# One more wait ahead of every second indirect transfer, and four clears behind a norm's powers, in a hybrid encoder on one core

## The chip, the cores and the metric

The kernel runs on one core of one Trainium2 chip. The core has five engines that work beside each other: TensorE (PE, the matmuls), VectorE (DVE), ScalarE (ACT), GpSimd (POOL) and SyncE (SP, which here only issues transfers), and 16 DMA engines that move data between HBM and the on-chip memory. The metric is the device time of one execution in microseconds (us); lower is better. Engines wait for one another through semaphores: counters that an instruction or a transfer raises when it is done.

## The reference, cut to what matters

The program is a two-layer encoder on 256 tokens of width 1024. Each layer has a token mixer (layer 0: windowed attention; layer 1: chunked gMLP) and then a PEER block, a mixture over 16384 experts of which each token uses 16 in each of 8 heads:

```python
def peer(h, w_query, sub_keys, expert_down, expert_up):
    ...
    q = (x @ w_query).reshape(T, PEER_HEADS, 2, D_HALF)
    s = jnp.einsum('thcd,hckd->thck', q, sub_keys).astype(jnp.float32)
    s1, i1 = lax.top_k(s[:, :, 0], PEER_TOPK)
    s2, i2 = lax.top_k(s[:, :, 1], PEER_TOPK)
    cand = (s1[..., :, None] + s2[..., None, :]).reshape(T, PEER_HEADS, PEER_TOPK * PEER_TOPK)
    ...
    top_s, pos = lax.top_k(cand, PEER_TOPK)
    idx = jnp.take_along_axis(cidx, pos, axis=-1)
    gate = jax.nn.softmax(top_s, axis=-1).astype(h.dtype)
    ...
        a = jax.nn.gelu(jnp.einsum('cd,chkd->chk', xc, expert_down[ic]))
        return jnp.einsum('chk,chkd->cd', a * gc, expert_up[ic])
```

## The kernel before, in words

The kernel does not gather experts. It computes the down products of all 16384 experts for all tokens, multiplies them with a matrix of gates that is zero wherever an expert was not chosen, and runs the up product over all experts. The gates lie in HBM, one tensor per layer (`gates`, 128 x 128 x 256 floats, 16.8 MB). It is first cleared by 32 plain transfers of 512 KB that POOL issues (`clear`), and then POOL writes the chosen gates into it by indirect transfers (`scatter`, `indirect_dma_start`). An item is one head of one half of the tokens, so there are 16 items a layer; each item takes 16 indirect transfers, each of one float for each of 128 tokens. That makes 256 indirect transfers a layer and 512 in all.

All weights arrive in **units** of 128 x 1024 floats (512 KB). SP loads a unit into one of four `raw` buffers; ACT makes its high half (`split_hi`, L465), DVE the low half (`split_lo`, L719), PE multiplies with both (three matmuls per product) and raises the semaphore `used` by one when it is through with the unit. Units are counted through the whole program: layer 0 has 20 units for the mixer, 16 for the query, 128 for down and 128 for up; layer 1 has 72, 16, 128 and 128. A query or down unit is 24 matmuls of 256 columns. ACT evicts the product of each query unit (L630) and of each down unit (L646).

While PE works on the query and the down units, DVE finds the 16 best experts of one item after the other (the search, 7 down units an item, until down unit 100), between its `split_lo`s. An item's indirect transfers wait for its gates (`gate_done`) and its addresses (`named`, made by ACT), and for the landing of the item before of the same tokens (`added`). At the end of the down stage SP waits for `added` before it loads the first gates for the up stage.

Ahead of each projection stands an RMS norm. DVE and ACT make the mean square, POOL raises it to the power -1/2 (`root`, L373, one small instruction for each half of the tokens), DVE scales, and PE turns the tiles. POOL is one queue in program order: in layer 0 the two powers of the second norm stand behind all 32 clears, and behind the powers stand the store of `h` to HBM (`h_kept`, L426) and the scatter. DVE's copy of the first key scores (L1085, first of the query stage) waits until that store has landed. Then come the loads for layer 1, which wait for units of the up stage.

What sets the order is thus the program order on each engine and these waits; there is no planner. The functions that the change touches are these.

Of the kernel before, what the change touches and what calls it, by code (L numbers as in the profile page):

```python
# [28 lines left out]
PH, TOPK, NK = 8, 16, 128  # L29
# [8 lines left out]
ZERO_UNITS = 4  # L38
TURN_ORDER = (0, 2, 1, 3, 4, 6, 5, 7)
FILL = 16  # L40
G_TILES = 4
RMS_EPS, LN_EPS = 1e-6, 1e-5
MASKED = -1.0e30
# [8 lines left out]
ATTN_UNITS, SG_V_UNITS, SG_UNITS, QUERY_UNITS = 20, 24, 72, 16  # L52
# [34 lines left out]
def build(nc, x, attn_units, sg_units, query_units, down_units, up_units, sub_keys, rel_table, bucket_map, sink,  # L87
# [5 lines left out]
    with ExitStack() as ctx:  # L93
# [3 lines left out]
        def sem(name):  # L97
            return ctx.enter_context(nc.semaphore(name))
# [16 lines left out]
        sums = sb("sums", [P, 2])  # L115
        g_t = [sb(f"g_t{s}", [P, T]) for s in range(G_TILES)]
        gains = sb("gains", [P, 2 * DEPTH, KD])
# [90 lines left out]
        used = sem("used")  # L208
# [51 lines left out]
        added = [[sem(f"added{n}_{t}") for t in range(TT)] for n in range(DEPTH)]  # L260
        g_landed = [sem(f"g_landed{s}") for s in range(G_TILES)]
        gated_up = sem("gated_up")
# [8 lines left out]
        unit0, p10 = [], []  # L271
# [18 lines left out]
        def _(sp):  # L290
# [24 lines left out]
            for layer in range(DEPTH):  # L315
# [8 lines left out]
                def up_gates(c, i):  # L324
                    sp.wait_ge(gated_up, i * GROUP + (layer * NK + c - G_TILES + 1))
                    sp.dma_start(g_t[c][:, :], gates[layer][bass.ds(i * GROUP + c, 1), :, :].rearrange("o p t -> (o p) t")
# [21 lines left out]
        @block.gpsimd  # L348
        def _(pool):
            pool.memset(ident[:, :], 0.0).then_inc(made, 1)  # L350
            pool.wait_ge(made, 1)
            pool.memset(neg_half[:, :], -0.5).then_inc(made, 1)
            pool.wait_ge(made, 2)
            pool.memset(table[BUCKETS:BUCKETS + 1, :], 1.0).then_inc(made, 1)
            pool.wait_ge(made, 3)
            pool.affine_select(out=ident[:, :], in_=ident[:, :], compare_op=ALU.not_equal, fill=1.0,
                               base=0, pattern=[[-1, P]], channel_multiplier=1).then_inc(made, 1)
            pool.memset(zeros[:, :], 0.0).then_inc(made, 1)
            pool.iota(token[:, :], [[1, 1]], base=0, channel_multiplier=1,
                      allow_small_or_imprecise_dtypes=True).then_inc(made, 1)  # L360
            pool.iota(place[:, :], [[1, TOPK]], base=0, channel_multiplier=0,
                      allow_small_or_imprecise_dtypes=True).then_inc(made, 1)
            pool.dma_start(gains[:, :, :], mix_g).then_inc(const_landed, 16)
            pool.dma_start(sink_in, sink.partition_broadcast(P)).then_inc(const_landed, 16)
            n = [0]

            def root(t):

                n[0] += 1
                if n[0] > 1:  # L370
                    pool.wait_ge(rstd_done, n[0] - 1)
                pool.wait_ge(ms_done, n[0])
                pool.tensor_tensor(stat[:, 1, t], stat[:, 0, t], neg_half[:, t], ALU.pow).then_inc(rstd_done, 1)  # L373

            def roots():
                for t in range(TT):
                    root(slice(t, t + 1))

            def load_keys(layer):
                pool.dma_start(keys_t.rearrange("p n k -> p (n k)"), sub_keys[layer]).then_inc(keys_landed, 16)  # L380

            def clear(layer, chunks, at):

                for q in chunks:
                    pool.wait_ge(used, at(q))
                    pool.dma_start(gates[layer][ZERO_UNITS * q:ZERO_UNITS * q + ZERO_UNITS].rearrange("i p t -> p i t"),  # L386
                                   zeros[:, :].rearrange("p (o t) -> p o t", o=1).broadcast_to([P, ZERO_UNITS, T])
                                   ).then_inc(zeroed, 16)

            def scatter(layer):  # L390

                pool.wait_ge(zeroed, 16 * (layer + 1) * (NK // ZERO_UNITS))
                flat = bass.AP(gates[layer].tensor, 0, [[1, NK * P * T], [1, 1]])
                for m in range(ITEMS):
                    t, head = m % TT, m // TT
                    pool.wait_ge(gate_done, ITEMS * layer + m + 1)
                    pool.wait_ge(named, ITEMS * layer + m + 1)
                    if head:
                        pool.wait_ge(added[layer][t], 16 * TOPK * head)
                    for k in range(TOPK):  # L400
                        pool.indirect_dma_start(flat, bass.IndirectOffsetOnAxis(address[:, TOPK * m + k:TOPK * m + k + 1], 0),  # L401
                                                whole[:, t, head, k:k + 1], None, element_offset=P * t
                                                ).then_inc(added[layer][t], 16)

            roots()

            pool.wait_ge(bias_row_done, 1)
            pool.dma_start(bias_rows, bias_row_sb[0:HEADS, :]).then_inc(bias_stored, 16)
            pool.wait_ge(bias_stored, 16)
            pool.dma_start(bias, bass.AP(bias_rows.tensor, 0, [[1, P], [4 * P, HEADS], [1, KEYS]])  # L410
                           ).then_inc(bias_landed, 16)
            pool.wait_ge(used, 8)
            load_keys(0)
            pool.wait_ge(made, 7)
            for layer in range(DEPTH):
                if layer == 0:
                    clear(0, range(NK // ZERO_UNITS), lambda q: 7 + 13 * q // 32)
                else:
                    roots()
                    at = unit0[1]["mix"]  # L420
                    clear(1, range(8), lambda q: at + 2 + 2 * q)
                    root(slice(0, TT))
                    clear(1, range(8, 32), lambda q: at + SG_V_UNITS + 4 + q)
                roots()
                pool.wait_ge(h_done, 4 * (2 * layer + 1))
                pool.dma_start(h_kept, h.rearrange("p t d -> p (t d)")).then_inc(h_stored, 16)  # L426
                scatter(layer)

                up = unit0[layer]["up"]
                if layer == 0:  # L430
                    at = up + HALF
                    for q in range(4):
                        c = slice(q * FF // 4, (q + 1) * FF // 4)
                        for where, what in ((g_bc[:, c], ln_g[c].partition_broadcast(P)),
                                            (b_bc[:, c], ln_b[c].partition_broadcast(P)),
                                            (wsp.rearrange("p j q -> p (j q)")[:, c],
                                             w_spatial.rearrange("p j q -> p (j q)")[:, c])):
                            pool.wait_ge(used, at)
                            pool.dma_start(where, what).then_inc(sg_landed, 16)  # L439
                            at += 3  # L440
                    for q in range(4):
                        c = slice(q * FF // 4, (q + 1) * FF // 4)
                        pool.wait_ge(used, at)
                        pool.dma_start(bsp.rearrange("p j q -> p (j q)")[:, c], b_spatial[c].partition_broadcast(P)
                                       ).then_inc(sg_landed, 16)
                        at += 3
                    pool.wait_ge(used, up + KEYS_COLUMN + 16 * NK // T)
                    load_keys(1)
                for t in range(TT):
                    pool.wait_ge(used, up + H_COLUMN + (t + 1) * (D // T))  # L450
                    pool.dma_start(h[:, t, :], h_kept[:, t * D:(t + 1) * D]).then_inc(h_landed, 16)  # L451
                if layer:
                    pool.dma_start(gain_row, final_g.partition_broadcast(P)).then_inc(gain_landed, 16)
            roots()
# [253 lines left out]
        def _(dve):  # L708
# [72 lines left out]
            for layer in range(DEPTH):  # L781
# [416 lines left out]
                def gate(n, i=0):  # L1198

                    dve.wait_ge(g_landed[n % G_TILES], i * 16 + 16 * (layer * NK // G_TILES + n // G_TILES + 1))  # L1200
                    a = acts[:, bass.ds(i * GROUP + n, 1), :]
                    dve.tensor_tensor(a, a, g_t[n % G_TILES][:, :].rearrange("p (o t) -> p o t", o=1), ALU.mult  # L1202
                                      ).then_inc(gated_up, 1)
# [84 lines left out]
        def _(pe):  # L1288
# [39 lines left out]
            def fill(bank):  # L1328

                for k in range(FILL):  # L1330
                    pe.transpose(psum[:, bank, P * (k % 4):P * (k % 4) + P], x_lo[:, k % KD, P:T].bitcast(F32), ident[:, :])
# [283 lines left out]
```

## Time and profile before

| | |
|---|---|
| median of 3 runs | 2186.74 us (2177.4 to 2198.01) |
| the profiled execution's own time | 2200.02 us |
| its span | 2198.2 us |
| PE busy | 1969.8 us, 90% |
| DVE busy | 1381.5 us, 63% |
| ACT busy | 1005.4 us, 46% |
| POOL busy | 664.3 us, 30% |
| mean granted TensorE clock | 0.934 of full |

Busy time of PE is modelled and overlaps itself; at a busy PE of 90% there may still be time in which few matmuls start. The page's slices split the span in 40 parts of 55 us. "Issue" as a releaser is time in which the engine waited for nothing that the profile shows, and "another core or an unknown queue" is a releaser that the profile can't name. On one core the latter is some queue or sequencer of the same core.

### The profile page before, as it was taken

The numbers are of one execution on the slowest core, as the hardware profiler recorded it, in microseconds if no ns is written. First come the engines' busy times: TensorE is split into PE (matmuls) and PEld (weight loads), VectorE is DVE, ScalarE is ACT, GpSimd is POOL, SyncE is SP. The second block draws the span as 40 slices with busy tenths as digits, with TensorE's granted clock in tenths as the row PEclk, the third lists the DMA queues.
The fourth block names the chain that finished last, engine by engine and source line by source line (L and its number), as shares of the span: only waits on it lengthen the run. The fifth ranks groups of instructions, "written<-read, shape, count | busy, mean of one in ns | idle before, by whom it ended". The sixth has DMA issues, their size and how long they took to land.

```text
span 2198.2 us, 38688 instructions
## 1 busy us (share of the span) xinstructions
PE 1969.8 (90%) x12114; PEld 1769.0 (80%) x12114; DVE 1381.5 (63%) x2970; ACT 1005.4 (46%) x1638; POOL 664.3 (30%) x627
## 2 busy tenths in 40 slices
PE   7978788777979999999999988789688799999998
PEld 6777688777979888888889988689588798888887
DVE  6856466456635766676567766467466535667776
ACT  5633354334535455444434444445254344554454
POOL 2324656656720000000102024666745620000000
PEclk9988898788989999999999998799798999999999
DMA  6943344333536877888749743344243356777775
GB/s 223 384 151 119 121 144 137 113 118 122 172 124 203 253 243 245 290 287 267 247 158 318 258 145 121 110 150 150 93 144 124 122 165 221 243 241 240 242 242 195
DMA packets 159588, 419.97 MB, mean 191 GB/s; under 512 B 32428, under 2 KB 66252, under 8 KB 159021
## 3 DMA queue, kind: packets, MB, share of 16 engines
q1 hardware_dynamic: 130556, 369.23, 52.1%
q0 software_dynamic: 28976, 50.17, 6.7%
q8 instruction: 16, 0.26, 0.1%
q14 instruction: 40, 0.32, 0.0%
HBM read 382.30 MB, written 37.00 MB: 191 GB/s over the span
## 4 chain that ended last, share of the span: by engine, by line
PE 77%; issue 7%; another core or an unknown queue 6%; ACT 5%; DVE 3%; DMA 2%; POOL 0%; SPq 0%; DVEq 0%; POOLq 0%; ACTq 0%
PE psum L1291 25%; PE psum L1293 25%; PE psum L1292 24%; ACT w_hi L465 2%; DVE w_lo L719 1%; ACT L614 1%; DMA big<-bias_rows 1%; PE psum L1490 1%; ACT L656 1%; PE psum L1461 1%; PE psum L1390 0%; PE psum L1379 0%; PE psum L1416 0%; DMA raw<-in_attn_units 0%
## 5 line engine op out<-in xcount | busy, mean ns | idle before, releaser
L719 DVE TENSOR_TENSOR w_lo<-raw,w_hi 128x1024 fp32r<-128x1024 f32 x636 | 772.5, 1219 | 452.4 <-ACT w_hi L465 341.2
L1291 PE MATMUL psum<-x_hi,w_hi 128*128 128x256 f32 x2576 | 767.0, 298 | 116.1 <-issue 68.5
L465 ACT CAST w_hi<-raw 128x1024 fp32r<-128x1024 f32 x636 | 662.5, 1047 | 345.1 <-PE psum L1293 328.1
L1292 PE MATMUL psum<-x_lo,w_hi 128*128 128x256 f32 x2576 | 753.7, 293 | 36.9 <-issue 36.4
L1293 PE MATMUL psum<-x_hi,w_lo 128*128 128x256 f32 x2576 | 754.1, 293 | 30.3 <-issue 29.7
L401 POOL DMA_INDIRECT gates<-whole,address x512 | 590.5, 1153 | 418.3 <-DVE whole L1073 167.3
L1291 PEld LDWEIGHTS psum<-x_hi,w_hi 128*128 128x128 f32 x2576 | 517.6, 201 | 142.5 <-issue 97.3
L1292 PEld LDWEIGHTS psum<-x_lo,w_hi 128*128 128x128 f32 x2576 | 518.8, 201 | 41.5 <-issue 40.4
L1293 PEld LDWEIGHTS psum<-x_hi,w_lo 128*128 128x128 f32 x2576 | 517.9, 201 | 39.5 <-issue 39.5
L1291 PE MATMUL psum<-w_hi,l_hi 128*128 128x512 f32 x1152 | 452.6, 393 | 3.4 <-DVE l_lo L1218 2.2
L1293 PE MATMUL psum<-w_hi,l_lo 128*128 128x512 f32 x1152 | 449.2, 390 | 0.0
L1292 PE MATMUL psum<-w_lo,l_hi 128*128 128x512 f32 x1152 | 449.0, 390 | 0.0
L646 ACT ACTIVATE big<-psum 128x256 f32<-128x256 f32 x256 | 98.1, 383 | 556.0 <-PE psum L1293 279.4
L1291 PEld LDWEIGHTS psum<-w_hi,l_hi 128*128 128x128 f32 x1152 | 216.9, 188 | 49.2 <-issue 4.4
L1293 PEld LDWEIGHTS psum<-w_hi,l_lo 128*128 128x128 f32 x1152 | 216.7, 188 | 45.8
L1292 PEld LDWEIGHTS psum<-w_lo,l_hi 128*128 128x128 f32 x1152 | 216.9, 188 | 43.8
L1207 DVE TENSOR_TENSOR l_lo<-big,l_hi 128x256 fp32r<-128x256 f32 x248 | 105.5, 426 | 190.7 <-ACT l_hi L664 190.7
L451 POOL DMA_DIRECT2D big<-h_kept x4 | 2.2, 551 | 418.8 <-PE psum L1293 418.8
L1202 DVE TENSOR_TENSOR big<-big,g_t 128x256 f32 (+1 forms) x248 | 104.0, 419 | 8.1 <-DMA g_t<-gates 8.1
L386 POOL DMA_DIRECT2D gates<-zeros x64 | 48.1, 755 | 183.3 <-PE psum L1293 160.4
L664 ACT CAST l_hi<-big 128x256 fp32r (+1 forms) x248 | 98.0, 396 | 0.0
L439 POOL DMA_DIRECT2D big<-in_ln_g x4 | 2.2, 548 | 270.1 <-PE psum L1293 270.1
(143 smaller groups left out, 1133.0 us busy)
## 6 DMA issues: line engine op xcount, KB each, us to landing
raw<-in_down SPq DMA_DIRECT2D x256, 512.0 KB
raw<-in_up SPq DMA_DIRECT2D x256, 512.0 KB
raw<-in_sg_units SPq DMA_DIRECT2D x72, 512.0 KB
gates<-zeros POOLq DMA_DIRECT2D x64, 512.0 KB, 7.4
g_t<-gates SPq DMA_DIRECT2D x248, 128.0 KB, 4.2
raw<-in_query SPq DMA_DIRECT2D x32, 512.0 KB
raw<-in_attn_units SPq DMA_DIRECT2D x20, 512.0 KB
gates<-whole,address POOLq DMA_INDIRECT x512
```

The source lines that it names most:

```text
L386: pool.dma_start(gates[layer][ZERO_UNITS * q:ZERO_UNITS * q + ZERO_UNITS].rearrange("i p t -> p i t"), zeros[:, :].rearrange("p (o t) -> p ...
L401: pool.indirect_dma_start(flat, bass.IndirectOffsetOnAxis(address[:, TOPK * m + k:TOPK * m + k + 1], 0), whole[:, t, head, k:k + 1], None, ...
L465: act.copy(w_hi[n % SPLIT][:, :], raw[n % RAW][:, :]).then_inc(hi_done, 1)
L614: act.activation(vals[:, item % 2, :], top1[:, item % 2, :], ACT.Exp, bias=least[:, item % 2:item % 2 + 1], accum_out=sums[:, item % 2:ite ...
L646: act.activation(acts[:, bass.ds(i * group + n, 1), :], p1[n % 2].rearrange("p (o t) -> p o t", o=1), ACT.Gelu_apprx_tanh).then_inc(p1_rea ...
L664: act.copy(l_hi[n % GROUP][:, :].rearrange("p (o t) -> p o t", o=1), acts[:, bass.ds(i * GROUP + n, 1), :]).then_inc(l_hi_done, 1)
L719: dve.tensor_tensor(w_lo[n % SPLIT][:, :], raw[n % RAW][:, :], w_hi[n % SPLIT][:, :].bitcast(F32), ALU.subtract).then_inc(lo_done, 1)
L1202: dve.tensor_tensor(a, a, g_t[n % G_TILES][:, :].rearrange("p (o t) -> p o t", o=1), ALU.mult).then_inc(gated_up, 1)
L1207: dve.tensor_tensor(l_lo[n % GROUP][:, :].rearrange("p (o t) -> p o t", o=1), acts[:, bass.ds(i * GROUP + n, 1), :], l_hi[n % GROUP][:, :] ...
L1291: pe.matmul(out_ap, hi_s, hi_m, start=start, stop=False)
L1292: pe.matmul(out_ap, hi_s, lo_m, start=False, stop=False)
L1293: return pe.matmul(out_ap, lo_s, hi_m, start=False, stop=stop)
```

## The change

Two edits, both in POOL's program. In `scatter` a wait for `used` now stands ahead of every second indirect transfer (even k): the transfers k and k+1 of item m wait until PE has finished 5 + 17 (16 m + k) // 32 units of the query and down stages. In layer 0 the last four of the 32 clears move behind the two powers of the second norm; they now wait for the end of the mixer's units (`ATTN_UNITS`, 20) where the last four had waited for 18 and 19. Layer 1's clears stay as they are.

```diff
@@ -38,6 +38,7 @@
 FILL = 16
+PACE_FROM, PACE_UNITS, PACE_WRITES = 5, 17, 32
 G_TILES = 4
@@ -398,6 +399,8 @@
                     if head:
                         pool.wait_ge(added[layer][t], 16 * TOPK * head)
                     for k in range(TOPK):
+                        if k % 2 == 0:
+                            pool.wait_ge(used, unit0[layer]["query"] + PACE_FROM + PACE_UNITS * (TOPK * m + k) // PACE_WRITES)
                         pool.indirect_dma_start(flat, bass.IndirectOffsetOnAxis(address[:, TOPK * m + k:TOPK * m + k + 1], 0),
                                                 whole[:, t, head, k:k + 1], None, element_offset=P * t
                                                 ).then_inc(added[layer][t], 16)
@@ -414,7 +417,7 @@
                 if layer == 0:
-                    clear(0, range(NK // ZERO_UNITS), lambda q: 7 + 13 * q // 32)
+                    clear(0, range(28), lambda q: 7 + 13 * q // 32)
                 else:
@@ -422,6 +425,8 @@
                     clear(1, range(8, 32), lambda q: at + SG_V_UNITS + 4 + q)
                 roots()
+                if layer == 0:
+                    clear(0, range(28, NK // ZERO_UNITS), lambda q: ATTN_UNITS)
                 pool.wait_ge(h_done, 4 * (2 * layer + 1))
```

POOL's instructions in layer 0 from the clears to the start of the scatter, before (DMA rows of `gates` from `zeros` are clears, those from `whole` indirect transfers, `stat` the powers):

```order
L386 DMA gates<-zeros 128x4x256 [waits used,made]
L386 DMA gates<-zeros 128x4x256 [waits used] x31
L373 TENSOR_TENSOR stat<-stat,neg_half 128x1 [waits ms_done,rstd_done] x2
L426 DMA h_kept<-big 128x2048 [waits h_done]
L401 DMA gates<-whole,address 4194304x1 [waits named,gate_done,zeroed]
L401 DMA gates<-whole,address 4194304x1 x15
```

The same place now:

```order
L387 DMA gates<-zeros 128x4x256 [waits used,made]
L387 DMA gates<-zeros 128x4x256 [waits used] x27
L374 TENSOR_TENSOR stat<-stat,neg_half 128x1 [waits ms_done,rstd_done] x2
L387 DMA gates<-zeros 128x4x256 [waits used] x4
L431 DMA h_kept<-big 128x2048 [waits h_done]
L404 DMA gates<-whole,address 4194304x1 [waits named,used,gate_done,zeroed]
L404 DMA gates<-whole,address 4194304x1
L404 DMA gates<-whole,address 4194304x1 [waits used]
```

The powers stand behind 28 clears and ahead of 4; the store of `h` and the scatter stay behind all 32, and after each two indirect transfers a wait for `used` stands where 15 had followed one another. No other engine's instructions change in number or order.

## Rows read from the trace of the kernel before

**Rows 1.** The page: span, and busy tenths and granted clock in 40 slices.

```profile
span 2198.2 us, 38688 instructions
...
POOL 2324656656720000000102024666745620000000
PEclk9988898788989999999999998799798999999999
```

**Rows 2.** The page: the chain that ended last, by engine.

```profile
PE 77%; issue 7%; another core or an unknown queue 6%; ACT 5%; DVE 3%; DMA 2%; POOL 0%; SPq 0%; DVEq 0%; POOLq 0%; ACTq 0%
```

**Rows 3.** Windows: stretch, length, busy us (x starts) of PE, PEld, DVE, ACT, POOL, clock, DMA.

```profile
289.00:317.90 28.90, 28.73 (x238) 28.33 (x236) 19.97 (x68) 17.95 (x29) 23.66 (x18) 1.00 0.51 164
317.90:339.00 21.10, 10.98 (x48) 9.09 (x48) 6.52 (x18) 3.33 (x9) 14.70 (x14) 0.69 0.23 75
551.90:590.10 38.20, 37.94 (x315) 37.55 (x314) 28.86 (x50) 24.20 (x41) 29.26 (x24) 1.00 0.56 178
640.00:697.00 57.00, 55.92 (x460) 55.49 (x459) 25.49 (x26) 27.41 (x44) 0.00 (x0) 1.00 0.56 184
...
1571.60:1596.30 24.70, 7.68 (x22) 5.32 (x21) 2.79 (x11) 0.04 (x1) 16.19 (x17) 0.50 0.08 22
```

**Rows 4.** Timeline of ACT: first query and last down eviction of each layer.

```profile
128.04 0.37 ACT L630 COPY big<-psum 128x256 f32<-128x256 f32 x1 [0.30 <-PE psum L1293]
...
694.35 0.38 ACT L646 ACTIVATE big<-psum 128x256 f32<-128x256 f32 x1 [1.56 <-PE psum L1293]
...
1278.88 0.37 ACT L630 COPY big<-psum 128x256 f32<-128x256 f32 x1 [0.30 <-PE psum L1293]
...
1841.67 0.38 ACT L646 ACTIVATE big<-psum 128x256 f32<-128x256 f32 x1 [1.56 <-PE psum L1293]
```

**Rows 5.** Windows of L646 alone: evictions of down units that start in the stretch.

```profile
551.90:590.10 38.20, 4.99 (x14) 1.00 0.56 178
640.00:697.00 57.00, 7.29 (x20) 1.00 0.56 184
```

**Rows 6.** Line L401, and timeline of POOL between 307 and 319 us, and the last of layer 0.

```profile
L401 POOL DMA_INDIRECT gates<-whole,address x512: 952/958/2933, 153.6 to 1778.3; - x171
...
307.21 0.96 POOL L401 DMA_INDIRECT gates<-whole,address  x1 [0.30 <-issue]
...
316.92 0.96 POOL L401 DMA_INDIRECT gates<-whole,address  x1 [0.30 <-issue]
318.18 0.95 POOL L401 DMA_INDIRECT gates<-whole,address  x1 [0.30 <-issue]
...
621.81 0.95 POOL L401 DMA_INDIRECT gates<-whole,address  x1 [0.30 <-issue]
```

**Rows 7.** The chain, in order of time: start, length, what.

```profile
368.91 3.83 another core or an unknown queue
```

**Rows 8.** Timeline of POOL at the end of layer 0's mixer.

```profile
101.17 0.75 POOL L386 DMA_DIRECT2D gates<-zeros  x1 [4.84 <-PE psum L1293]
118.00 0.75 POOL L386 DMA_DIRECT2D gates<-zeros  x1 [16.08 <-issue]
...
119.92 0.59 POOL L426 DMA_DIRECT2D h_kept<-big  x1
```

**Rows 9.** Timeline of DVE there: scaling, first copy of scores.

```profile
119.37 1.75 DVE L753 TENSOR_SCALAR big<-big,stat 128x512 f32<-128x512 f32 x4 [11.43 <-POOL stat L373]
...
131.37 0.42 DVE L1085 COPY big<-psum 128x256 f32<-128x256 f32 x1 [2.36 <-PE psum L1490]
```

**Rows 10.** Windows there, columns as in Rows 3.

```profile
101.90:116.00 14.10, 4.75 (x28) 3.98 (x28) 5.05 (x10) 3.04 (x6) 0.02 (x1) 0.83 0.92 352
116.00:119.90 3.90, 0.00 (x0) 0.00 (x0) 0.53 (x2) 0.00 (x0) 1.80 (x3) 0.50 0.17 61
```

**Rows 11.** Landing of L426's stores (min/median/max), and SP's first gate loads, second half of tokens.

```profile
DMA to landing us min/median/max: 4.2/4.2/4.2
...
690.59 2.12 SPq L336 DMA_DIRECT2D g_t<-gates  x4
```

## The prediction, as it was put on record before the changed kernel was run

> **What bounds the kernel now.** I read the page's slices first, then the chain, then windows over the stages where POOL works, and the timelines last. PE carries 77% of the chain, but 13% of it are "issue" and "unknown queue" [rows 2], some 285 us of 2198. The slices say where: the granted clock is at its lowest where POOL is busiest, in the slices 3 to 12 and 25 to 31, counted from 1, and nowhere else for long [rows 1]. Those are the query and down stages of the two layers, in which POOL issues the indirect transfers.
>
> The windows show that such a stage has two speeds. From 640.0 us, with no indirect transfer, 20 down units are evicted in 57.0 us [rows 3, 5], which is 2.88 us a unit (20 evictions and most of a unit at the edges). From 551.9 to 590.1 POOL starts 24 indirect transfers, and 14 evictions, the first and last at its edges, bound 13 units in 38.2 us: 2.94 us a unit at full clock [rows 3, 5]. So indirect transfers as such cost PE next to nothing. But from 317.9 to 339.0 PE starts 48 matmuls, two units, in 21.1 us, while POOL starts 14 transfers; and from 1571.6 to 1596.3 it is 22 matmuls in 24.7 us, at 0.50 of the clock, which is the 1.2 GHz level, with 8% on the DMA engines, while POOL starts 17 [rows 3]. I call these **pauses**. In a pause neither PE, ACT nor DVE gets on, DMA is not the bound, and POOL alone runs on, one transfer each 1.26 us where it is quickest [rows 6].
>
> What do all pauses share? They begin after a run of quick transfers. Ahead of the one at 317.9 POOL went from 307.21 to 318.18 with 9 transfers, 1.37 us each and the last at 1.26 [rows 6]; in the 28.9 us up to there it had 18, 1.61 us each, without harm [rows 3]. And they feed on themselves: nothing in the program stops POOL within an item when PE stands.
>
> What do they cost? First query to last down eviction takes 566.3 us in layer 0 and 562.8 in layer 1 [rows 4], for 143 steps. Without pauses I make it 15 query steps at some 3.35 us (50; an estimate, a down unit plus two small matmuls and the copies, between 2.9 and 3.7), 100 down units with search at 2.94 (294) and 28 at 2.88 (81): 425 us. The pauses cost 141 and 138 us, 279 in all.
>
> **The change, part by part.** *The pace.* 17 units for 32 transfers are, at 2.94 us a unit, one transfer per 1.56 us (24 in 38.2 us were 1.59). That is about the mean rate at which the harmless stretches ran, so the wait doesn't slow the scatter much; what it takes away are the runs at 1.26 us, and the going on while PE stands: when PE pauses, POOL has two transfers left (2.5 us) and then waits itself. 256 transfers take 5 + 17 x 254 / 32, so the last pair goes when 139 of the 144 units are through, and the pauses, on this theory, never build up. I leave small ones: the chain has a unit with 3.83 us of waiting at 368.91 [rows 7] which cost 2.3 us over a normal step; five of them in a layer (one for each three items) are 12 us. Gain 2 x (140 - 12) = **256 us**. Bounds: at the least nothing (the pauses have another cause), at the most 279.
>
> What is queued behind the new waits? On POOL, after the scatter, only loads that wait for units of the up stage, far later. Whoever waits for the scatter is SP, which issues the first gate loads of the second half of the tokens at 690.59, while the last transfer had started at 621.81 [rows 6, 11]: 68 us of slack. Now the last pair starts five units before the last eviction, at 694.35 - 5 x 2.88 = 679.9 on the old scale; two transfers, 2.5 us, and a landing, for which I take 4.2 us as for the store [rows 11], make 686.6. The last items are of the second half of the tokens, for which SP asks at 690.59. So 4 us of cover are left where there had been 68; nothing is added to the path, and each us of POOL's lag beyond it would be.
>
> The 256 waits themselves (128 a layer) I cost at nothing: POOL is not on the chain [rows 2]. PE's `used` is raised anyway.
>
> *The four clears.* POOL issued clear 31 of 32 at 101.17, and then stood 16.08 us until 118.00 for the last one, which took 0.75 us, and only then came the two powers [rows 8]. The reason for the stand is not named; the DMA engines were 92% busy until 116 and 17% after [rows 10], so it went as the backlog of clears drained. DVE was through with the mean squares at 107.94 and waited 11.43 us for the powers, with PE idle [rows 9, 10]. With the powers first, POOL waits for nothing there but the mean square, and PE starts 11.4 us sooner, the most to be had. Some comes back. Four clears (2 MB) now queue when PE starts again, and the last of them again waits for the drain, now against weight loads that want 512 KB per 2.9 us: I take the store of `h` from 119.92 to 121.5, so that it lands at 125.7. The first copy of scores, which needs it, stood at 131.37 [rows 9] and would come at 119.9. It waits 6 us; PE has two more units' operands by then (5.8 us less 1.6 for the copy and the low half that it then needs), so 2 us show. Net gain **9 us**, between 4 and 11.4. That the scatter starts behind the clears costs nothing: it began at 153.6 [rows 6].
>
> **Sum.** 2200.0 - 9 - 256 = 1935. The profiled execution is 13 us above the median of the runs, and I take pauses to differ from run to run by about that; with few left, runs should be nearer together. I say **1930 us**.
>
> **The rivals.**
> *Cut pauses* (B). The pace is no slower than POOL goes unhindered (1.56 against 1.59 to 1.61 us), so with DVE's larger steps POOL may lag and then catch up in a run of 1.26 us. A transfer took 0.952 to 2.933 us [rows 6], so it is held up at times. The Trainium skill's page "SBUF — State Buffer" ("Who interferes with whom") has it that a DVE instruction with two SBUF inputs and a GpSimd one that reads SBUF shut each other out; the spread agrees, and would leave such lags. For it: most pauses came within some 20 transfers of a burst's start. Against: 24 in a row ran clean. Then a pause would start once in each search of 7 units, 14 times a layer, but end after POOL's two transfers (2.5 us) and one unit at half clock (2.3 us more): 5 x 14 = 70 us a layer, 2200 - 9 - 2 x 70 = **2051 us**.
>
> *The pauses are not POOL's* (C). The Trainium skill's page "SBUF — State Buffer" says in the same section that DMA never contends with a compute engine and that PE and ACT never wait on anyone; by it the pace brings nothing, and what coincides with POOL's bursts would be the search. What speaks for it from rows is that PE's operands are in place and the DMA engines idle at 8%, so that no bandwidth is short [rows 3]. Against it: in 551.9 to 590.1 the search ran in full and there was no pause. Then only the norm is left: 2200 - 9 = **2191 us**.
>
> *Each pair has a price* (D), the other side. If a pause is what a fresh start of transfers costs (the small one of 2.3 us), 128 pairs a layer would each pay it where 16 items had: 294 us a layer instead of 140, so 2200 - 9 + 2 x 154 = **2499 us**; a part of the pairs gives a part of it. The point from which it decides is 140 / 128 = 1.1 us a pair. Against it: POOL's items that began after a gap, at 289.0 and 551.9, cost nothing in the 28 us that followed [rows 3]. The same side is reached if the scatter outlasts the down stage, but 4 us of cover and 1.3 us a transfer of lag make that a matter of tens of us at most.
>
> **Chances.** Pauses gone or nearly so 0.62, B 0.22, C 0.09, D 0.07. Range: all pauses gone and the full 11.4 is 1909, less 1% for runs that lay that far below the profile: 1890. At the top it takes in B and something beyond its 2051, 2090; C and D stay out. What a measurement here can tell from no change is about 1%, 22 us. Faster by more: 0.62 + 0.22 = 0.84; within: C, 0.09; slower by more: D, 0.07.
>
> **What would show it.** In the changed profile the granted clock stays near 1.0 through both query and down stages, the first query to last down evictions take some 437 us, POOL's transfers come in pairs spread evenly, with waits put down to PE, and the "unknown queue" share of the chain falls from 6% to about 1%. The scatter ends some five units before the down stage and SP's first gate loads are not late. DVE's wait for the powers is near 1 us, and its first copy of scores waits some 5 us for the store. I would be wrong if PE's pauses stand with POOL waiting in them (C), if each pair is followed by a slow unit (D), or if PE waits at the start of the up stage.

## The result and the profile after

On the chip of the first comparison the changed kernel takes 2000.72 to 2012.48 us, median 2008.97 of 4 runs, against 2182.07 (2172.72 to 2198.01, 4 runs) before: ratio 0.9194 [0.913, 0.9259]. Its profiled execution took 2000.72 us, 199.3 less than the one before. In four later groups, on four chips, the kernel before itself took only 1940 us; the changed kernel was run in two of them and was 0.4 and 0.2% faster, the second not clear of noise. (Which chip the first comparison ran on is not on record, so it may be one of the four.) So there are two parts to explain: what the change did where there were pauses, and why they were there at all. Times are compared below only within one group of runs on one chip, and where a stage of one group is set against another's, the text says so. The ratios leave out executions more than 1.5% above the fastest of their kernel, so they need not be the quotient of the medians.

The page after, slices of 50 us (compare [rows 1]), and the chain by engine (compare [rows 2]):

```profile
span 1998.9 us, 38718 instructions
...
POOL 1416687777650000000102105687777740000000
PEclk9998998999999999999999999998999999999999
...
PE 87%; DVE 4%; issue 3%; ACT 3%; another core or an unknown queue 2%; DMA 1%; POOL 0%; SPq 0%; DVEq 0%; POOLq 0%; ACTq 0%
```

The clock row has lost its 7s. "Issue" and "unknown queue" together fell from 13% of the chain to 5%.

Timeline of ACT after, the first query and the last down eviction of each layer (the rows that answer to [rows 4]):

```profile
117.22 0.37 ACT L635 COPY big<-psum 128x256 f32<-128x256 f32 x1 [0.30 <-PE psum L1298]
...
594.17 0.38 ACT L651 ACTIVATE big<-psum 128x256 f32<-128x256 f32 x1 [1.56 <-PE psum L1298]
...
1176.04 0.37 ACT L635 COPY big<-psum 128x256 f32<-128x256 f32 x1 [0.30 <-PE psum L1298]
...
1643.20 0.38 ACT L651 ACTIVATE big<-psum 128x256 f32<-128x256 f32 x1 [1.56 <-PE psum L1298]
```

The two stages now take 477.0 and 467.2 us where they took 566.3 and 562.8: 185 of the 199 us. The first query eviction comes 10.8 us sooner. All other stretches together give the remaining 3.5.

Pauses are left. Windows over the two largest of layer 0 (start:end, length, then busy us and starts of PE, PEld, DVE, ACT and POOL, clock, DMA):

```profile
300.60:317.40 16.80, 8.67 (x48) 7.65 (x48) 5.09 (x17) 5.80 (x9) 12.52 (x13) 0.80 0.25 81
148.00:175.00 27.00, 22.28 (x136) 20.91 (x135) 14.69 (x50) 5.61 (x9) 16.50 (x16) 0.75 0.33 103
```

In the first, PE started two units' matmuls (48) in 16.8 us while POOL started 13 transfers. I had said that POOL would have two left and then wait. POOL's timeline there, and the counts of transfers (L404) and of down and query evictions (L651, L635) up to 295.4 us and up to 316 us, tell why it did not:

```profile
304.24 0.95 POOL L404 DMA_INDIRECT gates<-whole,address  x1 [0.30 <-issue]
305.50 0.96 POOL L404 DMA_INDIRECT gates<-whole,address  x1 [0.30 <-issue]
...
L651 ACT ACTIVATE big<-psum x35: 378/385/387, 190.0 to 291.4; 128x256 f32<-128x256 f32 x35
L635 ACT COPY big<-psum x16: 365/372/373, 117.2 to 185.4; 128x256 f32<-128x256 f32 x16
L404 POOL DMA_INDIRECT gates<-whole,address x81: 952/962/2535, 149.1 to 295.4; - x81
...
L651 ACT ACTIVATE big<-psum x38: 378/385/387, 190.0 to 306.5; 128x256 f32<-128x256 f32 x38
L404 POOL DMA_INDIRECT gates<-whole,address x96: 952/961/2535, 149.1 to 315.8; - x96
```

Transfer 81 wants 5 + 17 x 80 / 32 = 47 units; 16 + 35 = 51 had been evicted, four to spare. Transfer 96 wants 54, and 16 + 38 = 54 was just what there was. The scatter had fallen behind its own pace, so the waits asked for nothing, and the credit of four units let it run through a whole pause at 1.26 us a transfer. Only then did the waits bind, and no later pause of this layer is as long.

The second window is the same thing at the scatter's start. The first transfer, at 149.1 us, wants 5 units, and 8 had been evicted; the three units of credit are used up by the eleventh transfer, and from there to the end of the second item the counts are met with at most one unit to spare. Set against the changed kernel on a chip without pauses (`after_again`, below), eviction by eviction, the query stage lost 10.2 us there and the four units from 291.4 us on 12.8; in layer 1 the query stage lost 8.6 and six units from 1376.2 us on 15.0 us. All four together are 47 us. The rest of what is left, 19 us in layer 0 and 14 in layer 1, is spread over the units behind, where the waits bind.

### The profile page after: what moved, and what is told of

Read it like the earlier page. It is cut to its first block, busy times and chain, and to the rows that moved or that the text cites. A ratio compares the mean times of both kernels' runs of the same rounds, so it can differ in the third digit from the quotient of the medians.

```text
span 1998.9 us, 38718 instructions
## 1 busy us (share of the span) xinstructions
PE 1906.0 (95%) x12114; PEld 1726.5 (86%) x12114; DVE 1381.4 (69%) x2970; ACT 1002.5 (50%) x1638; POOL 701.7 (35%) x627
## 4 chain that ended last, share of the span: by engine, by line
PE 87%; DVE 4%; issue 3%; ACT 3%; another core or an unknown queue 2%; DMA 1%; POOL 0%; SPq 0%; DVEq 0%; POOLq 0%; ACTq 0%
PE psum L1296 28%; PE psum L1298 28%; PE psum L1297 27%; DVE w_lo L724 1%; ACT w_hi L470 1%; PE psum L1495 1%; PE psum L1466 1%; PE psum L1384 0%; ACT L619 0%; DVE big L781 0%; PE psum L1395 0%; PE psum L1421 0%; ACT L661 0%; DMA raw<-in_attn_units 0%
## 5 line engine op out<-in xcount | busy, mean ns | idle before, releaser
L1296 PE MATMUL psum<-x_hi,w_hi 128*128 128x256 f32 x2576 | 749.6, 291 | 55.2 <-issue 22.6
L1298 PE MATMUL psum<-x_hi,w_lo 128*128 128x256 f32 x2576 | 739.7, 287 | 3.6 <-issue 3.3
L1297 PE MATMUL psum<-x_lo,w_hi 128*128 128x256 f32 x2576 | 739.6, 287 | 2.2 <-issue 2.0
L404 POOL DMA_INDIRECT gates<-whole,address x512 | 627.2, 1225 | 302.6 <-issue 147.4
L1296 PEld LDWEIGHTS psum<-x_hi,w_hi 128*128 128x128 f32 x2576 | 504.8, 196 | 72.0 <-issue 40.2
L1298 PEld LDWEIGHTS psum<-x_hi,w_lo 128*128 128x128 f32 x2576 | 504.8, 196 | 4.9 <-issue 4.9
L1297 PEld LDWEIGHTS psum<-x_lo,w_hi 128*128 128x128 f32 x2576 | 505.1, 196 | 4.1 <-issue 2.9
L651 ACT ACTIVATE big<-psum 128x256 f32<-128x256 f32 x256 | 98.4, 385 | 381.0 <-PE psum L1298 266.8
```

What stands on the lines that cost most here:

```text
L651: act.activation(acts[:, bass.ds(i * group + n, 1), :], p1[n % 2].rearrange("p (o t) -> p o t", o=1), ACT.Gelu_apprx_tanh).then_inc(p1_rea ...
L1296: pe.matmul(out_ap, hi_s, hi_m, start=start, stop=False)
L1297: pe.matmul(out_ap, hi_s, lo_m, start=False, stop=False)
L1298: return pe.matmul(out_ap, lo_s, hi_m, start=False, stop=stop)
```

## The experiments

The label "before" in what follows is the kernel before, run on the same chip beside the others. **With pauses** were the first comparison and the last group of runs here; all other groups were **without pauses**, and there before takes 1938 to 1940 us. So no kernel with only one of the two edits was measured with pauses.

### Each edit alone, the waits always met, and no transfers (one chip, without pauses)

**The pace alone**: the clears as before.

```diff
-                    clear(0, range(28), lambda q: 7 + 13 * q // 32)
+                    clear(0, range(NK // ZERO_UNITS), lambda q: 7 + 13 * q // 32)
 ...
-                if layer == 0:
-                    clear(0, range(28, NK // ZERO_UNITS), lambda q: ATTN_UNITS)
```

> The waits for units are in, the four clears stay ahead of the norm's powers. Pauses come from runs of quick indirect transfers that nothing stops (theory F, feedback): the two query and down stages take about as long as in the changed kernel (477 and 467 us from first query to last down eviction), so 2020 us against 2009 with both edits. Rival C (the pauses are not POOL's): within 1% of 2182.

Measured: 1943.3 us (10 runs) against 1940.4 (25 runs), ratio 1.0013 [0.9995, 1.0031]. The stages take 427.9 and 428.1 us, with no pause. The timeline of ACT at their ends in layer 0:

```profile
129.47 0.37 ACT L633 COPY big<-psum 128x256 f32<-128x256 f32 x1 [0.29 <-PE psum L1296]
...
557.35 0.38 ACT L649 ACTIVATE big<-psum 128x256 f32<-128x256 f32 x1 [1.56 <-PE psum L1296]
```

So where there are no pauses the pace is worth nothing, and a stage without them takes 428 us: my 425, put together from single steps, stands.

**The clears alone**: the changed kernel without its pace.

```diff
-                        if k % 2 == 0:
-                            pool.wait_ge(used, unit0[layer]["query"] + PACE_FROM + PACE_UNITS * (TOPK * m + k) // PACE_WRITES)
```

> The four clears stand behind the norm's powers, the waits for units are out. All theories: DVE gets the powers some 10 us sooner; its first copy of scores waits for the store of h. Net 8 us under before, 2174 us; if the scatter's pauses have more to do with the start than thought, anything between 2160 and 2190. The pauses stay at some 280 us for both layers.

Measured: 1935.67 us, 0.9975 [0.9956, 0.9995]. Stages 434.2 and 428.2. The edit gains 4.7 us: some 11 us ahead of the stage, less 6.3 within layer 0's.

**Both edits, but each wait is for a count long reached**, so that the instructions are there and never hold POOL.

```diff
-                            pool.wait_ge(used, unit0[layer]["query"] + PACE_FROM + PACE_UNITS * (TOPK * m + k) // PACE_WRITES)
+                            pool.wait_ge(used, unit0[layer]["query"] + PACE_FROM)
```

> Both edits, but the wait ahead of every second transfer is for query unit 5 alone, so it is always met: the same number of waits that never hold. Theory F: as clears_only, about 2174 us, with the pauses back. A rival (the waits as such, as instructions between the transfers, thin them out): near 2009 us.

Measured: 1935.89 us, 0.9973 [0.9953, 0.9993]; the same as without the instructions. The wait instructions themselves cost nothing that can be seen, as I had taken them. The rival, that they thin the transfers out, had no pauses here to shorten and stays untested.

**No indirect transfer at all** (the chosen experts' part is left out, and SP no longer waits for `added`):

```diff
                     for k in range(TOPK):
-                        pool.indirect_dma_start(...)
+                        pass
```

> All 512 indirect transfers are left out, with their waits, so the gates stay zero and the experts' part of the output is missing; SP waits for the search and the clears instead. What all pauses cost: theory F expects 427 us for each query and down stage and a total of 2009 - (477 + 467 - 2 x 427) = 1919 us. Rival C (pauses are the search's or the fetching of instructions): the pauses stay, 2009 us or above.

Measured: 1920.14 us (2 runs), 0.9891 [0.9856, 0.9927]; stages 433.4 and 428.1, as with the transfers. Without pauses, then, 512 transfers cost some 15 us against the clears alone, and next to none of it within the stages. In the two profiles, 14.3 us apart, the stretch from layer 0's last down eviction to layer 1's first query eviction is 4.6 us shorter without transfers, and the one behind layer 1's last down eviction 9.6. What stands there is shown by the next group. With no pauses to lose, this run says nothing on what makes them (rival C).

### Before and after once more (two other chips, without pauses)

> The changed kernel once more, since in the runs so far the kernel before took 1940 us where the profile before had 2200, with no pauses at all. Theory P (the pauses belong to a chip or its state, and the pace shortens them only where they are): where before takes 2182 us, this takes 2009; where before takes 1940, this takes 1943 less the norm's 5 to 9, 1936 us. Rival (the pace gains in itself): well under 1936 where before takes 1940.

Measured: 1931.36 us against 1938.74, 0.9963 [0.9949, 0.9978].

> The kernel before once more, for a profile where it takes 1940 us. Theory P (the pauses are a state of the chip): every unit as in the profile before where that had no pause, 2.9 us, with 16 indirect transfers an item and the same runs at 1.26 us; first query to last down eviction 428 us. Rival: fewer quick runs, so that POOL itself is slower here. If before takes 2182 here, the pauses are in the profile as before.

> The changed kernel on the same chip as before_again. Without pauses 7 us under it (0.996); with pauses 2009 us against 2182.

Measured, on a further chip: before 1940.26 against itself 1939.53, 1.0004 [0.9981, 1.0028]; after 1935.36, 0.9983 [0.9957, 1.0009]. Here is a page of the kernel before without pauses, its slices and its chain, word for word the same program as [rows 1, 2]:

```profile
span 1938.1 us, 38688 instructions
...
POOL 1406688787750000000102106688787750000000
PEclk9989999999999999999999999999999999999999
...
PE 56%; POOL 29%; issue 9%; DVE 3%; DMA 2%; ACT 1%; SPq 0%; POOLq 0%; DVEq 0%; ACTq 0%
...
L401 POOL DMA_INDIRECT gates<-whole,address x512 | 643.5, 1257 | 241.7 <-issue 162.0
```

POOL, 0% of the chain with pauses, is 29% of it here. A transfer takes 1257 ns on the mean (1225 in the changed kernel with pauses) and 0.3 us lie between two, so an item of 16 takes some 25 us while the search hands over one each 20.6; from some 209 us on POOL goes nearly without a break (in layer 0 it stands only twice for more than 0.5 us between two transfers, for 2.3 and 1.9 us). The ends of the scatter, of the down stage and SP's first gate loads, from three timelines of the same kernel:

```profile
564.08 0.96 POOL L401 DMA_INDIRECT gates<-whole,address  x1 [0.30 <-issue]
...
556.11 0.38 ACT L646 ACTIVATE big<-psum 128x256 f32<-128x256 f32 x1 [1.55 <-PE psum L1293]
...
550.45 1.86 SPq L333 DMA_DIRECT2D g_t<-gates  x4
566.24 2.01 SPq L336 DMA_DIRECT2D g_t<-gates  x4
```

The last transfer starts 8 us after the last down eviction, and SP issues the loads of the gates of the second half of the tokens 15.8 us after those of the first. So the 15 us of the transfers lie behind the down stages, where the up stage waits for gates. It also says what the pace can't do here: it is one transfer per 1.56 us, about POOL's own rate, so POOL never gets ahead of it. In `after_again` the transfers run 4 to 7 units behind what the pace would allow for most of the stage, and no wait for PE ahead of one lasts over 0.3 us; in the changed kernel with pauses such waits reach 2.2 us.

The stage takes 427.9 and 428.2 us, as theory P expected, but the runs of quick transfers are not the same: never more than 6 starts in a row less than 1.35 us apart, where the profile with pauses has up to 15. A long quick run is thus at least in part what a pause makes. Once the search is over, the transfers start 1.26 and 1.62 us apart in turn, beside one low half of VectorE's per unit; in a pause VectorE stands, and they go at 1.26. The held scatter below shows which comes first.

### The store of h ahead of the late clears (same chip as after_again, without pauses)

```diff
-                if layer == 0:
-                    clear(0, range(28, NK // ZERO_UNITS), lambda q: ATTN_UNITS)
                 pool.wait_ge(h_done, 4 * (2 * layer + 1))
                 ...                       # the store of h
+                if layer == 0:
+                    clear(0, range(28, NK // ZERO_UNITS), lambda q: ATTN_UNITS)
```

> The changed kernel with the store of h ahead of the four late clears: DVE's 7.6 us of waiting for that store goes, and 3 to 6 us of it show, so 4 us under the changed kernel; the scatter starts no later. Were the store still late (behind the backlog of the 28 clears), no difference.

Measured: 1926.37 us, 0.994 [0.9913, 0.9966]; stage of layer 0 427.9 us, in the changed kernel on this chip 434.5. The timelines of POOL and DVE, first of the changed kernel:

```profile
109.44 1.50 POOL L374 TENSOR_TENSOR stat<-stat,neg_half 128x1 f32<-128x1 f32 x2 [17.08 <-DVE stat L734]
110.89 2.45 POOL L387 DMA_DIRECT2D gates<-zeros  x3
119.34 0.75 POOL L387 DMA_DIRECT2D gates<-zeros  x1 [5.99 <-issue]
120.08 0.55 POOL L431 DMA_DIRECT2D h_kept<-big  x1
...
126.86 0.42 DVE L1090 COPY big<-psum 128x256 f32<-128x256 f32 x1 [7.82 <-DMA h_kept<-big]
```

and then with the store first:

```profile
106.61 1.50 POOL L374 TENSOR_TENSOR stat<-stat,neg_half 128x1 f32<-128x1 f32 x2 [17.08 <-DVE stat L734]
108.07 0.59 POOL L429 DMA_DIRECT2D h_kept<-big  x1
108.65 1.67 POOL L387 DMA_DIRECT2D gates<-zeros  x2
115.05 1.50 POOL L387 DMA_DIRECT2D gates<-zeros  x2 [4.74 <-PE psum L1298]
...
118.38 0.42 DVE L1090 COPY big<-psum 128x256 f32<-128x256 f32 x1 [2.34 <-PE psum L1495]
```

In the changed kernel the last clear stood 6 us, the store went behind it, and DVE's first copy waited 7.8 us for its landing. With the store first it waits for PE alone, and the 6.5 us come back in the stage, 5.0 in the medians of the whole. The two kernels' intervals overlap a little; it is the stage in the traces that shows the gain.

### The pace again, on top of that (one chip, without pauses)

No pace at all (two lines fewer), and a wait ahead of every transfer:

```diff
-                        if k % 2 == 0:
+                        if True:
```

> The store of h ahead of the four late clears and no waits for units in the scatter. Where before takes 1940 us (no pauses), POOL is the bound of the scatter either way (256 transfers at 1.6 us, ending some 2 to 6 us behind the down stage), so the pace costs nothing and brings nothing: 1926 us, the ratio 0.994 of store_first. Where before takes 2182 the pauses are all there: some 2165 us.

> As store_first, with the wait ahead of every transfer in place of every second, same rate. Without pauses: 1926 us, or up to 10 us more if single transfers lag the pace further. With pauses (before 2182): theory F (runs of quick transfers) has shorter runs and less pause, 1960 to 1990 us; if the pauses left in the changed kernel come from late counts and not from pairs, 2005 us, as with pairs.

Measured against 1938.37: without the pace 1926.96 us, 0.9949 [0.993, 0.9968]; one wait a transfer 1924.13, 0.9931 [0.9911, 0.9952]. The intervals overlap; the finer pace costs nothing, and no complete kernel here has a lower median. What it is worth with pauses, the very thing it was made for, was not measured.

### The transfers held back, and half of them (last group, with pauses)

This group ran on the very chip of the last one, some twelve minutes later, and now before took 2207.36 us (2180.43 to 2222.27, 7 runs). **Held**: the kernel before, but the scatter waits until 100 down units are done; then 256 transfers stand ready, with the search over.

```diff
                 pool.wait_ge(zeroed, 16 * (layer + 1) * (NK // ZERO_UNITS))
+                pool.wait_ge(used, unit0[layer]["down"] + 100)
```

> The kernel before, whose scatter waits until 100 down units of its layer are through, when the search is over, and then runs all 256 transfers with nothing between them. Total about 2430 us (the up stage waits some 245 us a layer); what counts are the last 27 down units. Theory P (runs of quick transfers hurt PE only on a chip in the state of the first profile): they stay at 2.9 us each beside dozens of transfers at 1.26 us. Rival L (long runs hurt on every chip, and were merely missing from the profiles without pauses): pauses as in the profile before, units of 5 to 14 us.

Measured: 2581.86 us, one run. The stage of layer 0 in two windows, before and from the first transfer, and then in three windows of one unit each (columns as above):

```profile
129.44:476.60 347.16, 343.96 (x2826) 339.68 (x2825) 280.73 (x813) 205.41 (x341) 0.00 (x0) 1.00 0.54 174
476.60:881.20 404.60, 118.11 (x672) 106.05 (x670) 35.08 (x34) 37.02 (x57) 252.51 (x256) 0.58 0.13 37
...
538.00:603.80 65.80, 8.03 (x24) 6.39 (x24) 1.23 (x1) 1.32 (x3) 49.95 (x53) 0.50 0.04 8
603.80:671.00 67.20, 8.02 (x24) 6.38 (x24) 1.23 (x1) 1.29 (x3) 49.93 (x53) 0.50 0.04 8
671.00:738.30 67.30, 8.03 (x24) 6.38 (x24) 1.23 (x1) 1.41 (x3) 51.14 (x54) 0.50 0.04 8
```

With no transfer there is no pause: 347 us at full clock, search and all, on a chip with pauses (before, without pauses, takes the same for these units). With all transfers in one run a unit of 24 matmuls takes 67.2 us, in which some 53 transfers go, one each 1.27 us. The expected total (2430 us) and the expected units (5 to 14 us) were both far too low. The timeline of PE and POOL in one of these units, and of PE and ACT at its end:

```profile
621.33 0.96 POOL L402 DMA_INDIRECT gates<-whole,address  x1 [0.30 <-issue]
621.93 0.37 PE L1293 MATMUL psum<-x_lo,w_hi 128*128 128x256 f32 x1 [2.43 <-issue]
622.59 0.96 POOL L402 DMA_INDIRECT gates<-whole,address  x1 [0.30 <-issue]
623.33 0.29 PEld L1294 LDWEIGHTS psum<-x_hi,w_lo 128*128 128x128 f32 x1 [2.51 <-issue]
624.73 0.37 PE L1294 MATMUL psum<-x_hi,w_lo 128*128 128x256 f32 x1 [2.43 <-issue]
...
649.96 0.37 PE L1294 MATMUL psum<-x_hi,w_lo 128*128 128x256 f32 x1 [1.73 <-issue]
670.97 0.38 ACT L647 ACTIVATE big<-psum 128x256 f32<-128x256 f32 x1 [65.91 <-issue]
671.41 0.58 PE L1292 MATMUL psum<-x_hi,w_hi 128*128 128x256 f32 x1 [21.07 <-issue]
671.78 0.42 PE L1293 MATMUL psum<-x_lo,w_hi 128*128 128x256 f32 x1
```

A weight load and a matmul follow each other at 1.40 us, each on nothing that the profile shows. It is not the clock: the first 15 of a unit's 48 weight loads and matmuls start some 0.21 us apart, at the same 0.50, the other 33 mostly 1.40. Then PE stands 21 us, until ACT evicts the unit, which ACT too does only 20 us after PE's last matmul. 15 times 1.40 are 21.0: my reading is that PE's instructions come at one each 1.40 us throughout, and that 15 had gathered while PE stood. Why ACT is late as well is open. The pauses of [rows 3] look like this seen from afar.

The same place in the kernel before without pauses is the test of which comes first, pause or quick run, and of rival L. There too the search is over and the transfers follow one another without a break. First `before_again`, then `hold`, 23 us each:

```profile
476.00:499.00 23.00, 23.00 (x194) 23.00 (x193) 9.81 (x8) 10.52 (x17) 18.13 (x17) 1.00 0.56 183
...
476.60:499.60 23.00, 20.58 (x167) 19.94 (x165) 7.73 (x9) 7.90 (x12) 17.61 (x16) 1.00 0.47 142
```

17 and 16 transfers; without pauses every unit takes 2.88 us, and goes on so to the end of the stage, with pauses the third already takes 4.5. Up to there `hold` has not even two intervals in a row under 1.35 us; `before_again` has. So the same transfers at the same pace harm PE in the one state and not in the other, and the long runs at 1.26 us come after the first slow units, not ahead of them. Runs of 53 at 1.26 us were never seen without pauses, so what they would do there is not known.

With pauses it does not set in at once: the first units after 476.6 take 2.9, 3.0, 4.5, 4.4, 3.8 us, then 7.3, 12.1, 23.3 and 65.8, while POOL goes from 1.4 to 1.5 us a transfer to 1.27. And it does not end at once. The windows behind the last transfers:

```profile
809.00:836.00 27.00, 4.98 (x13) 3.73 (x13) 0.00 (x0) 0.00 (x0) 1.76 (x2) 0.50 0.06 19
840.00:880.00 40.00, 40.00 (x322) 40.00 (x322) 16.61 (x15) 17.46 (x27) 0.00 (x0) 0.96 0.56 182
```

PE starts 13 matmuls in the 27 us in which POOL has hardly anything left to issue, and then is itself again. From 813 to 835 us not one DMA packet of any queue is on record, so it isn't a backlog of data that PE waits for; what it is the traces do not show. The stage took 751.7 us in all, 323.8 more than 427.9, and 256 transfers at 1.27 us are 325. Once the pause has set in, PE all but stands as long as POOL issues without a break.

**Half**: the kernel before with 8 of the 16 transfers of each item (half of the chosen experts is left out), no pace; the counts of `added` that POOL and SP wait for are halved too.

```diff
-                    for k in range(TOPK):
+                    for k in range(TOPK // 2):
```

> The kernel before with 8 of each item's 16 indirect transfers, so half of the chosen experts is left out. Where before takes 1940 us: if the transfers cost time there only because the last ones end behind the down stage, the scatter ends in time and this takes 1940 - 15 = 1925 us or a little less. If each transfer slows PE, half of the 15 us stays: 1932 us. Where before takes 2182, fewer and shorter bursts: 2000 to 2080 us.

Measured: 1940.26 us (4 runs), 0.8851 [0.8774, 0.8928]. The stages, and the one long pause:

```profile
129.35:560.90 431.55, 424.81 (x3496) 420.13 (x3494) 317.14 (x846) 241.31 (x398) 163.02 (x128) 1.00 0.55 174
1142.70:1584.10 441.40, 429.94 (x3496) 424.41 (x3494) 317.33 (x845) 240.71 (x397) 161.41 (x128) 0.98 0.54 171
1340.00:1351.00 11.00, 7.77 (x43) 7.13 (x42) 6.50 (x18) 3.74 (x9) 2.59 (x3) 0.69 0.36 112
```

From eviction to eviction the stages take 431.3 and 441.4 us, so half the transfers leave 3.4 and 13.2 us of pauses where all of them made 138 and 135 in the first comparison. The state had not gone, as a step of 9.1 us in layer 1 shows. If each transfer had a price, half would be left; it is 6%. What the kernel before mostly lacked is the gap of some 9 us that now stands between the bursts of eight. Whether the gap counts or the length of the burst was not separated.

## Why the prediction was right, and where not

Predicted 1930 us and a gain of 265 in the profiled execution; measured 2008.97 and 199.3. That unbroken transfers make the pauses holds. Two terms were mis-sized, and two premises were wrong: that a pause needs a run of quick transfers ahead of it, and that the pauses belong to the kernel.

**The pauses.** That POOL's transfers make them, in the state with pauses, is now shown: held back, they vanish with the search running; let go in one run, PE all but stops; halved, 6% is left. Rival C is refuted with pauses, and its result, 2191 us, did not come. But its words hold without pauses, where taking out all 512 transfers leaves the stages as they are (chip of `no_transfers`). That "they begin after a run of quick transfers" is not so in `hold`: there the first slow units come while the transfers start 1.26 to 1.77 us apart, with no run in them, and `before_again` keeps that pace without harm. That it was the pace, and not the moved clears, that took 192 us of pauses away was not measured by itself; for it speak the traces, in which the waits bind from 316 us on, and that the clears act ahead of the stage. The Trainium skill's page "SBUF — State Buffer", section "Who interferes with whom", has it that DMA never contends with a compute engine and PE never waits on anyone. The profiles without pauses agree (units of 2.88 us beside unbroken transfers); the held scatter, at 67.2 us a unit, does not, and there the measurement decides. The section is about the ports of the on-chip memory, and nothing here shows that PE and POOL met at one.

**"POOL has two transfers left and then waits itself", and the 12 us a layer** is the step that failed. Taking 434.5 and 428.2 us (from `after_again`) as the changed kernel's stages without pauses, 42.5 and 39.0 us were left, 81 where I had 24. That is 57 of the 66 us by which the profiled gain was short. The pace is a count of units from the stage's start. It holds a POOL that is ahead of it, and gives credit to one that is behind: three units at its start and four at 295.4 us, a whole pause's worth. The two pauses on credit in each layer are 47 of the 81 us. Where the waits bind, 33 us remain in smaller ones of some 1 to 5 us. At the end of layer 0's down stage three evictions come late (steps of 5.9 us at 554, 564 and 576 us), but the next one or two steps are 1.2 to 2.4 us, so that each costs under 1 us. So even paced pairs leave something; whether late counts, which let several pairs go at once, or the transfers as such make it was not tested.

**What pauses cost before**: 279 us by my sum, 138.4 + 134.6 = 273 against the stages of 427.9 and 428.2 us that `before_again` measured.

**The norm.** 11.4 us at most was right (10.8 came, the first query eviction). I let 2 us of the store's landing show; 6.5 did (434.5 against 427.9). I had counted operands of two further units as cover for PE, but DVE makes the low halves of the weights behind that copy, in its program order, and PE stood: 6 matmuls start between 124 and 127 us in `after_again`, where 28 had in the 3 us before. Net 4.3 instead of 9; clears_only, without pauses, gained 4.7.

**The cover of 4 us.** With pauses it held: the last transfer started at 583.4, 11 us ahead of the last eviction. Without pauses it was never there, in the kernel before neither: in the nine such profiles with all transfers the scatter runs 2 to 8 us past the down stage. I had taken the 68 us of slack for a property of the kernel; it was time that the pauses had given to POOL.

**Rivals B and D.** The result lies between my forecast and B (2051), and what is left has B's form, lag and then a run at 1.26 us; its 14 pauses a layer of 5 us were 40 us instead of 70. D did not come: 128 pairs a layer left 42.5 and 39.0 us, at most 0.33 us a pair, against its 2.3 and the 1.1 from which it decides. (pace_only, 1.0013, shows the same without pauses.)

**What was not foreseen**: that the term of 279 us need not be there. The range of 1890 to 2090 held the time with pauses. That it also held the time without them was chance: nothing in the prediction speaks of a state in which the change is worth 0.4%.

## What to carry to other kernels

A wait on a count of the consumer's progress bounds only a producer that is ahead; where bursts do harm, limit the burst itself (so many after the last, or a count from the item's own start); that bursts of eight with a gap do little harm is shown here, a limit for all sixteen was not tried. Put whatever another engine waits for ahead of bulk transfers in the same queue. And before a stall that takes 13% of the time is tuned away, run the kernel on a second chip or at another time: here the same program took 2182 or 1940 us.

## What the runs showed of the hardware

- The same program runs with or without pauses: 2182.07 and 2207.36 us in two groups, 1938.37 to 1940.4 in four. One chip had both, 1938.37 and some twelve minutes later 2207.36. The chip alone does not set it; what does is open, and nothing tried here bears on it.
- With pauses, indirect transfers at 1.27 us without a break let PE start 48 weight loads and matmuls in 67.2 us, most of them 1.40 us apart. It takes some six units to set in, and PE is slow for 28 us after the last transfer. Without pauses the same unbroken transfers at 1.3 to 1.6 us cost PE nothing in 28 units of 2.88 us. Which resource they share was not found. The DMA engines were at 4%, and behind the last transfer idle, so it is not bandwidth; that it is the supply of instructions is what the equal 1.40 us steps, and the 15 that had gathered in 21 us, suggest, not more.
- In the same windows the granted clock is 0.50, its 1.2 GHz level, as PE starts 24 matmuls in 67 us; it is not the cause, since at that clock a matmul takes 0.37 us of each 2.80, and others start 0.21 us behind a weight load.
